# A hybrid decoder step on one Trainium2 core: the difference of two softmax maps is formed and stored in the joint stage, and the attention stage loads it, turns it and splits it

## What is computed

```python
def _diff_attn(q, k, v, q_pos, k_pos, slopes, lam):
    s = jnp.einsum('bqmhd,bkmhd->bmhqk', q, k, preferred_element_type=jnp.float32) * (DH_A ** -0.5)
    dist = (q_pos[:, None] - k_pos[None, :]).astype(jnp.float32)
    s = jnp.where(dist >= 0, s - slopes[:, None, None] * dist, NEG_INF)
    p = jax.nn.softmax(s, axis=-1)
    p = p[:, 0] - lam * p[:, 1]
    return jnp.einsum('bhqk,bkhd->bqhd', p.astype(v.dtype), v)
```

## Time and profile before

| what | value |
|---|---|
| device time, median of 3 runs | 2545.97 us (2540.29 to 2546.51) |
| span of the profiled execution | 2554.0 us |
| PE busy | 2459.9 us, 96% of the span |
| DVE busy | 1572.7 us, 62% |
| ACT busy | 910.6 us, 36% |
| mean granted clock of the matrix engine | 0.983 |

### The profile page before, as it was taken

The page is one execution under the profiler, slowest core; times in us unless marked ns, Lnnn a source line. Parts: engine busy times, 40 slices in busy tenths (PEclk is TensorE's granted clock), DMA queues, the critical chain, the costliest instruction groups (busy, mean ns, idle before and its releaser), DMA issues. The chain is left out here.

```text
span 2554.0 us, 34275 instructions
## 1 busy us (share of the span) xinstructions
PE 2459.9 (96%) x12691; PEld 1965.0 (77%) x12691; DVE 1572.7 (62%) x2540; ACT 910.6 (36%) x1449; POOL 186.4 (7%) x182
## 2 busy tenths in 40 slices
PE   5999999999999999999999999999999897999998
PEld 2788888887788878888888778877777654788886
DVE  3411336644676417778886788977877656655564
ACT  3211122225333228884001556644444433222221
POOL 0000112210232100000000200000000000000000
PEclk9999999999999999999999899999999998999999
DMA  8653645555455477764445866446466397545541
GB/s 305 231 192 146 226 133 165 165 167 203 139 159 141 143 228 195 200 162 126 146 144 142 178 150 149 96 82 133 93 137 156 116 320 269 170 144 149 144 141 55
DMA packets 296286, 417.51 MB, mean 163 GB/s; under 512 B 62624, under 2 KB 180136, under 8 KB 286581
## 3 DMA queue, kind: packets, MB, share of 16 engines
q1 hardware_dynamic: 283630, 382.18, 52.6%
q10 hardware_dynamic: 11456, 33.30, 3.5%
q0 software_dynamic: 1056, 0.13, 0.1%
HBM read 277.88 MB, written 137.65 MB: 163 GB/s over the span
## 5 line engine op out<-in xcount | busy, mean ns | idle before, releaser
L1884 DVE CUSTOM_DVE_ANT_0 max_s_ps<-max_s_ps,max_causal 128x128 f32<-128x128 f32 (+7 forms) x256 | 194.3, 769 | 70.0 <-PE max_s_ps L1942 50.8
L704 PE MATMUL proj_z<-first_km,h_hi 128*128 128x512 f32 x576 | 230.1, 399 | 3.2 <-DVE first_v L1276 3.2
L704 PE MATMUL proj_z<-first_km,h_lo 128*128 128x512 f32 x576 | 226.1, 393 | 0.0
L704 PE MATMUL proj_z<-first_v,h_hi 128*128 128x512 f32 x576 | 224.4, 390 | 0.0
L2267 ACT ACTIVATE att_b_pf<-att_b_s_ps 128x1024 f32<-128x1024 f32 (+2 forms) x160 | 142.4, 898 | 102.9 <-PE att_b_s_ps L2310 79.6
L1843 ACT ACTIVATE max_s_ps<-max_s_ps,max_neg_top 128x128 f32<-128x128 f32 (+2 forms) x192 | 161.2, 840 | 43.2 <-DVE max_neg_top L1884 31.6
L2284 DVE TENSOR_TENSOR att_b_p_lo<-att_b_pf,att_b_p_hi 128x1024 fp32r<-128x1024 f32 (+2 forms) x160 | 170.5, 1066 | 5.5
L1887 DVE TENSOR_REDUCE max_neg_top<-max_s_ps 128x1 f32<-128x1024 f32 x128 | 154.2, 1225 | 17.9 <-PE max_s_ps L1942 11.4
L2279 DVE CAST att_b_p_hi<-att_b_pf 128x1024 fp32r<-128x1024 f32 (+2 forms) x160 | 98.1, 613 | 70.0 <-ACT att_b_pf L2267 67.4
L1051 POOL TENSOR_TENSOR proj_rstd<-proj_rstd,keep_neg_half 128x8 f32<-128x8 f32 (+1 forms) x68 | 112.7, 1658 | 323.8 <-DVE proj_rstd L1374 323.8
L1242 ACT ACTIVATE proj_work<-proj_z 128x512 f32<-128x512 f32 x64 | 38.3, 598 | 270.3 <-PE proj_z L704 270.3
(11 more groups left out here) (475 smaller groups left out, 6148.2 us busy)
## 6 DMA issues: line engine op xcount, KB each, us to landing
w_raw<-in_w_in SPq DMA_DIRECT2D x144, 256.0 KB, 3.7
smp_v_a<-scratch_mixes SPq DMA_DIRECT2D x16, 1024.0 KB, 5.2
map_qm<-scratch_q_hi SPq DMA_DIRECT2D x48, 256.0 KB
map_k<-scratch_k_hi SPq DMA_DIRECT2D x37, 256.0 KB
head_w<-in_w_ada SPq DMA_DIRECT2D x8, 1024.0 KB, 6.8
scratch_mixes<-proj_out SPq DMA_DIRECT2D x32, 256.0 KB, 3.1
scratch_k_hi<-proj_work SPq DMA_DIRECT2D x32, 256.0 KB, 2.3
scratch_k_lo<-proj_work SPq DMA_DIRECT2D x32, 256.0 KB, 2.8
```

Source lines behind the costliest of these rows:

```text
L704: ins = nc.tensor.matmul(out, left(*lt), right(*rt), start=first and n == 0, stop=last and n == len(terms) - 1)
L1884: nc.vector.tensor_tensor_reduce(s, s, causal[:, 1024 - w:1024], -1.0, -NEG, ALU.add, ALU.min, accum_out=neg_top[:, kh, u, qt:qt + 1]).the ...
```

## The change

The exponentials of the differential attention are drawn once. In the joint stage (now `gates_and_maps`) the order is the 8 units of the forgetting attention first, then, for each head, tiles of 128 queries (0 to 7, then 15 down to 8), each with both maps and one or two tasks of keys. DVE takes the maximum over the whole row (the second task starts from the first one's result), then ACT draws the exponentials with the row's maximum into SBUF, map 0 into the ring `max_p0` (5 places of 1024), map 1 into `max_p1` (2 places). DVE then makes a reciprocal and a factor for the row and forms the difference of the maps in place (`combine`), and SP stores it in DRAM (`maps`, 4 heads x 2048 x 2048, of which the causal part is written). `attention_a` no longer computes scores: SP loads blocks of 512 queries x 512 keys (`att_a_maps`, 8 places), the matrix engine turns each 128 x 128 piece into `att_a_turned`, ACT copies it to the high part, DVE subtracts for the low part, and the products with the values stay. The scale of the row (one over the sum of map 0) is applied when a group is finished. The weights of the gates come in halves (front and back), and ACT's queue, not SP's, stores the output tiles.

```diff
-                nc.scalar.activation(s, s, ACT.Exp, bias=neg_top[:, kh, u, qt:qt + 1], scale=-1.0 if kh == qh else 1.0,
-                                     accum_out=sums[:, kh, u, qt:qt + 1]).then_inc(sum_done, 1)
+            def probabilities(x):
+                kind, g, qt, m, kh = tasks[x]
+                h, seg, both = rows[g][0], seg_of(g, kh), qt >= HALF
+                act.wait_ge(max_done, last_of(g, m) + 1)
+                if m == 0 and seg >= P0_RING:
+                    act.wait_ge(k.map_stored[seg % P0_RING], 16 * (seg // P0_RING))
+                if m == 1 and seg >= P1_RING:
+                    act.wait_ge(comb_done, seg - P1_RING + 1)
+                dst = p0[:, seg % P0_RING, 0:width[x]] if m == 0 else p1[:, seg % P1_RING, 0:width[x]]
+                total = parts[:, g % 4, kh, m:m + 1] if both else sums[:, h, qt, m:m + 1]
+                nc.scalar.activation(dst, scores(x), ACT.Exp, bias=neg_top[:, g % 4, m, both:both + 1],
+                                     scale=-1.0 if kh == qt // 8 else 1.0, accum_out=total).then_inc(exp_done, 1)
...
+            def factors(g):
+                h, qt = rows[g]
+                total, scale = sums[:, h, qt, :], k.scale_a[:, h, qt, :]
+                dve.wait_ge(exp_done, order[last_of(g, 1)] + 1)
+                if qt >= HALF:
+                    step.inc(nc.vector.tensor_tensor(total, parts[:, g % 4, 0, :], parts[:, g % 4, 1, :], ALU.add))
+                    step.wait(dve)
+                step.inc(nc.vector.reciprocal(scale, total))
+                step.wait(dve)
+                step.inc(nc.vector.scalar_tensor_tensor(factor[:, g % 4:g % 4 + 1], total[:, 0:1], k.neg_lam[:], scale[:, 1:2],
+                                                        ALU.mult, ALU.mult))
+            def combine(g, kh):
...
+                step.wait(dve)
+                nc.vector.scalar_tensor_tensor(first, p1[:, seg % P1_RING, 0:w], factor[:, g % 4:g % 4 + 1], first,
+                                               ALU.mult, ALU.add).then_inc(comb_done, 1)
...
+    for x, (kind, g, qt, m, kh) in enumerate(tasks):
...
+        if kind == "a":
+            top_a(x)
+            if m and g and kh == 0:
+                factors(g - 1)
+                finish(g - 1, [0] if qt >= HALF else [0, 1])
+            if m and g and kh == 1:
+                finish(g - 1, [1])
```

In `attention_a` (SP, ACT, DVE and the matrix engine in turn):

```diff
+                def load_block(b):
+                    h, g, kg = blocks[b]
+                    src = k.maps[h][g * 512:(g + 1) * 512, :].rearrange("(j p) s -> p j s", p=P)
+                    for j in range(copies[b]):
+                        js, w = (slice(j, j + 1), (j + 1) * P) if kg == g else (slice(0, GROUP), 512)
+                        sp.dma_start(maps[:, b % PIECES, js, 0:w], src[:, js, kg * 512:kg * 512 + w]).then_inc(maps_in[b % PIECES], 16)
+                map_pieces_stored(k, sp)
                 for done, count in k.max_out_stored:
                     sp.wait_ge(done, count)
...
+                    load_block(b)
+                    if b == 1:
+                        load_v(k, sp, 0, LO)
+                    if b == 3:
+                        for part in (HI, LO):
+                            load_v(k, sp, 1, part)
+                    if b == PIECES:
                         load_b(k, sp, 0)
...
-                    nc.scalar.activation(pf[:, n // 2 % PR, :, at:at + w], s_ps[:, n % PLACES, :, 0:w], ACT.Exp,
-                                         bias=a.bias[h % 2][:, col:col + 1]).then_inc(p_done, 1)
+                    nc.scalar.activation(p_hi[:, n % HR, 0:w], turned[:, n % PLACES, 0:w], ACT.Copy).then_inc(hi_done, 1)
...
+                    nc.vector.tensor_tensor(p_lo[:, n % HR, 0:w], turned[:, n % PLACES, 0:w], p_hi[:, n % HR, 0:w].bitcast(F32),
+                                            ALU.subtract).then_inc(lo_done, 1)
...
+                    for x in range(count):
+                        last = nc.tensor.transpose(turned[:, n % PLACES, x * P:(x + 1) * P],
+                                                   maps[:, b % PIECES, GROUP - count + x, kt % 4 * P:(kt % 4 + 1) * P], k.ident[:])
```

909 lines of the change are left out of this document (477 added, 432 removed).

## The result

The changed kernel takes 2637.3 us (median of 4 runs, 2636.5 to 2638.0), the kernel before on the same chip 2546.2 us: 1.036 times the time, 95% interval 1.034 to 1.037. The forecast was 2567 with 2612 as the upper end. The direction was right; the size, 91 us for the 21 forecast, was off by a factor of four.

A forecast was written before the change was run, and what follows sets the result against it. The matrix engine bounds the joint stage and `attention_a` before. After: joint stage 381 + 5 + 168 + 11 = 565 us, `attention_a` with gap 193, sum 758 for 737: +21 us, median 2567 us, range 2537 to 2612.

The forecast's parts named there:

- 66.5 + 66.5 + 1067 x 0.23 + 3 = 381: Joint stage up to the third head: forgetting scores, two differential heads' scores, 1067 products and a slow start, 381 us.
- I add 5 us for places where it waits for a bank: Joint stage ahead of the third head: the matrix engine, still the bound there, idles 5 us in sum.
- 79 us: Vector work of one differential head: maxima 45, differences 23.2 and small operations 10.8 us.
- Few tenths a tile, 5 us for a head: Third and fourth heads: waits for held banks add 5 us to a head's vector work, making 84 us.
- The near tie for tile 15: Differential heads: exponential, its read and next scores take 2.3 us while the vector engine has 2.5 us to do.
- I don't take it as the likely case: Last two heads at half clock: 11 us more a head, 95 us each; set aside as only a bound.
- T: Time of the two heads without products: 168 us forecast, 148 without waits, 190 as the half-clock bound.
- attention_a 193 us: `attention_a` with its gap: transfers 189 us, more than the matrix engine's 172, plus some 4 us before they start.
- the rival of the starved start: `attention_a`: early values and forgetting loads starve the matrix engine; A = 210, T = 180, 2596 us; chance 0.15.
- T + A under 337: Condition for 0.3% faster: heads without products plus `attention_a` with gap (A) below 337 us; forecast 366 with the 5 us.
- The page's figure of 358 GB/s: `attention_a`: at this HBM share 53.5 MB take 149 us, so the matrix engine's 172 us would decide.
- The rival of the half clock in `attention_a`: Turns don't keep the clock up, products and turns take 310 us of the stage; 2716 us; chance 0.05.

The follow-up runs named there:

- experiment 3: The changed kernel, but each exponential is drawn with the maximum of its own task, not of the row (long rows of the result wrong); 2632.9 us.
- the eleventh kernel: The tenth with 24 products behind the last task in place of 48; 2533.5 us, 0.9935 of the kernel before.
- the ninth: The changed kernel with later key loads, stored maps from GpSimd's queue, later `attention_a` loads and four result places, forgetting vector work costed at 0.9; 2578.1 us (1.011).
- the eighth: The changed kernel with forgetting vector work costed at 0.9 and the products spread evenly over the four differential heads; 2602.7 us.
- experiment 4: The changed kernel with some values, keys and queries loaded later in `attention_a`, and four places for results in place of two; 2627.9 us (1.032).
- experiments 4 and 5: The second of the two: the changed kernel with four places for results in place of two, loads as they were; 2631.7 us (1.033).
- the first edit of the plan: The changed kernel with the planner costing forgetting vector work at 0.9, so 529 products stand ahead of the first head for 614; 2625.1 us.
- the tenth: The ninth with products spread evenly over the differential heads and forgetting vector work costed at 0.8; 2546.1 us, 0.999 of the kernel before.

## Why the forecast was wrong, point by point

- **"66.5 + 66.5 + 1067 x 0.23 + 3 = 381", the matrix engine's work up to the third head: right.** Measured 386.5 us busy.
- **"I add 5 us for places where it waits for a bank": the first step that failed.** The idle time there is 18.6 us, in a stretch where I counted banks and no transfer. 10.5 of it stand in the second head, where the matrix engine waited 10.3 us for queries (31.1 in sum, less 20.8 in the last two heads). Of the 5.5 us in the first head, 4.1 are one wait for ScalarE.
- **Vector work of a head, "79 us": a little high.** The difference of 1024 elements takes what was priced, in the view of groups of the changed kernel:

```profile
L2016 DVE SCALAR_TENSOR_TENSOR max_p<-max_p,max_factor 128x1024 f32<-128x1024 f32 x40 | 51.4, 1284 | 1.3
L2007 DVE SCALAR_TENSOR_TENSOR max_factor<-max_sums,keep_neg_lam,scale_a 128x1 f32<-128x1 f32 x64 | 14.0, 220 | 2.4
L2005 DVE RECIPROCAL scale_a<-max_sums 128x2 f32<-128x2 f32 x64 | 10.4, 163 | 1.2
```

  The small operations take 0.16 to 0.22 us each; a head's vector work is 71 to 74 us.
- **"Few tenths a tile, 5 us for a head": the step that failed most.** It was meant for banks, and as that it holds: experiment 3 gives 4 to 5 us a head. But it stood for all waits of a head, and the vector engine idles for 23 us in one. I had costed the joint stage's edits on three engines and left out SP's queue, whose order the change makes decisive: before, the matrix engine waited for nothing (466.8 of 467.0 us), now ScalarE waits for a stored map and the matrix engine for queries behind keys. About 10 us of the 23 are the wait for queries (20.8 us in the two heads). In the eleventh kernel, where no wait for queries is left, 9 us of idle time stay in each of the last two heads, the banks' 4 to 5 probably among them. The 4 to 7 us between are what missing products and the clock cost together (below). This split is worked out from differences between runs; no run shows it as a whole. The near tie for tile 15 was also closer than I wrote: the terms 1.09 + 0.19 + 4 x 0.23 + 0.3 make 2.5 us, not 2.3, which leaves nothing to the vector engine's 2.5.
- **"I don't take it as the likely case", the clock: wrong.** It was 0.62 and 0.55 of full in the last two heads. The working had a slip that made this case look safer: the "133 us of work" are the scores of all four heads. Two heads have 66.5 us and the 37 products 8.5, so 75 us in 168, and the stretch that I took as evidence, busy for 74.7 of 84 us, was a much fuller one. The size of the bound, 11 us a head, was not reached: with transfers in order the ninth and the eleventh kernel differ in their last two heads by 7.1 and 5.4 us, at a clock of 0.80 and 0.54 against 1.00 and the same vector work (71.6 to 72.0 against 70.6 to 72.1 us). With late queries in both, the changed kernel and the eighth differ by 4.5 and 3.8 us, at 0.62 and 0.55 against 0.91. Both pairs also differ in how many products stand between the scores; no experiment changed the clock alone, so 4 to 7 us is a price for missing products and clock together. That T came out at 191 us, next to the bound of 190 that rests on the clock, is chance: that bound had no late transfer in it.
- **"attention_a 193 us": the mechanism was right, one part of the risk came true.** The transfers do set the stage: with loads in a better order it takes 193.5 us for the 193 forecast, with a DMA share of 0.99 over the stage's 185.7 us (experiment 4). As the change stands it takes 210.6, what the rival of the starved start had as A = 210. Its reason, values and keys among the first blocks, is 12 us by experiments 4 and 5; the places of the results, 4.5 us, I had not seen.
- **The page's figure of 358 GB/s** (the Trainium skill, DMA: Bandwidth & Descriptors, Specifications) would have left 172 us, the matrix engine's. For the stage as a whole the traces don't agree: the DMA engines are 0.99 busy and move 291 GB/s in the eleventh kernel. Single stretches do get there, 369 GB/s in the row of the fourth experiment.
- **The rival of the half clock in `attention_a`: excluded.** From 1660 us on, in a stage that the forecast counted as 40% turns, the granted clock is 1.00:

```profile
1660.00:1680.00 20.00, 20.00 (x129) 17.10 (x128) 11.63 (x20) 10.71 (x22) 0.00 (x0) 1.00 1.03 329
1680.00:1700.00 20.00, 20.00 (x141) 17.89 (x140) 13.57 (x24) 11.71 (x23) 0.00 (x0) 1.00 0.97 306
```

  By the Trainium skill (TensorE: Matmul & The Clock Gate, Part 4: PE-mode transpose) a transpose doesn't count as work for the clock in the way that a matmul does; no run here has transposes alone, and this stage, with turns among products, kept the clock.

So for the balance that asked for T + A under 337, T is 191 us in place of 168 and A 210.6 in place of 193, and ahead of the third head the change lost 19 us for 5. The change can pay, but not alone: of the 104 us between it and the eleventh kernel, 59 came with the ninth (by their times alone 18.1 and 9.4 for the order of transfers and the places, 8.1 for GpSimd's queue, 12.2 for the first edit of the plan), 32 with the even plan of the tenth, and 12.6 with the last step, whose cause is open. Such a plan has nothing to give to the kernel before, whose matrix engine has no hole in this stage. And the gain at the end is small: 0.9935 of its time.

## What to carry to other kernels

When work moves to another stage, cost the queue that issues its transfers as you cost an engine: list what stands ahead of each load that an engine waits for, and ahead of each store that frees a buffer. Filling work (here products of another matrix) belongs evenly between the steps that are bound by another engine; in front of them it only lengthens the program. And a stage with full DMA engines can starve the matrix engine or not, by what it loads first.

## What the runs showed of the hardware

- Issues take time on the queue that makes them: a key or query transfer of 64 rows takes 0.6 us of SP's queue, fifteen transfers (six of them smaller, 0.4 us) 8.7 us. In `attention_a` five issues of maps held the queue for 18 us, and a result's store stood behind. One of the five took 14.5 us (from 1590.5 on), though the turns that free its place had ended at 1577.7; what held it isn't shown:

```profile
1588.98 0.40 SPq L2159 DMA_DIRECT2D scratch_o_a<-att_a_o  x1
1589.43 17.96 SPq L2166 DMA_DIRECT2D att_a_maps<-scratch_maps  x5
1607.43 0.55 SPq L2159 DMA_DIRECT2D scratch_o_a<-att_a_o  x1
```

- The mean granted clock was 0.55 in a head where the matrix engine shows 63.5 busy of 95.3 us, and 1.00 in one with 74.9 of 79.8 us.
- A stage that mostly reads maps in rows of up to 2 KB moved 291 GB/s over 184 us with the DMA engines busy for 0.99.
